# The MLP's up projections in a three-layer block: high and low part of h in one moving operand

## The reference

```python
def sq_relu_mlp(h, w1, w2):
    return jnp.square(jax.nn.relu(h @ w1)) @ w2      # w1: 1024 x 4096, w2: 4096 x 1024

# in each of the first two layers
h = rmsnorm(x, g[2])
x = x + rmsnorm(sq_relu_mlp(h, mlp_w1[l], mlp_w2[l]), g[3])
```

## Time and profile before

| | us |
|---|---|
| median of 3 runs (lowest, highest) | 912.43 (911.15, 913.14) |
| profiled execution, its time | 911.07 |
| profiled execution, span in the trace | 909.3 |
| PE busy in the span | 898.6 (99%) |
| DVE, ACT busy | 630.7 (69%), 483.4 (53%) |
| mean granted clock of PE | 0.997 of full speed |

### The profile page before, as it was taken

One profiled execution on the slowest core, in us unless ns is written; L12 is line 12 of the kernel. 1 busy time (PEld: TensorE's weight loads), 2 busy tenths in 40 slices (PEclk: granted clock), 3 DMA queues, 4 the chain that ended last, 5 costly groups with the idle time before them and its releaser, 6 DMA issues.

```text
span 909.3 us, 14541 instructions
## 1 busy us (share of the span) xinstructions
PE 898.6 (99%) x6258; PEld 796.2 (88%) x6258; DVE 630.7 (69%) x763; ACT 483.4 (53%) x639; POOL 33.6 (4%) x25
## 2 busy tenths in 40 slices
PE   8999999999999999999999999999999999999997
PEld 6989888899999998998889999999889998888885
DVE  5798746568666666689466867666678795456655
ACT  7775456465343334665566534334467784356624
POOL 0000000000000000000000000000000084000000
PEclk9999999999999999999999999999999999999999
DMA  9644544466666665544446666666445444334431
GB/s 352 238 171 139 179 142 142 140 215 226 231 231 231 232 232 185 176 173 139 139 139 215 229 228 232 236 233 233 149 168 209 140 139 141 98 112 145 140 133 46
DMA packets 24447, 165.47 MB, mean 182 GB/s; under 512 B 2720, under 2 KB 2976, under 8 KB 5184
## 3 DMA queue, kind: packets, MB, share of 16 engines
q1 hardware_dynamic: 22896, 159.72, 49.9%
q0 software_dynamic: 1056, 4.34, 1.3%
q10 hardware_dynamic: 432, 0.49, 0.2%
HBM read 163.49 MB, written 1.05 MB: 181 GB/s over the span
## 4 chain that ended last, share of the span: by engine, by line
PE 95%; DVE 2%; ACT 2%; DMA 1%; issue 0%; SPq 0%; DVEq 0%; ACTq 0%
PE acc L591 29%; PE lin L549 10%; PE lin L557 10%; PE lin L550 9%; PE lin L573 7%; PE lin L580 7%; PE lin L574 7%; PE acc L673 2%; PE acc L677 1%; PE acc L773 1%; PE acc L674 1%; PE lin L636 1%; PE acc L868 1%; DMA raw<-in_weights 1%; PE lin L651 1%; DVE w_lo L1792 1%
## 5 line engine op out<-in xcount | busy, mean ns | idle before, releaser
L1792 DVE TENSOR_TENSOR w_lo<-raw,w_hi 128x2048 fp32r<-128x2048 f32 x137 | 315.5, 2311 | 155.0 <-ACT w_hi L1309 154.4
L1309 ACT CAST w_hi<-raw 128x2048 fp32r<-128x2048 f32 x137 | 260.1, 1905 | 166.3 <-DMA raw<-in_weights 109.3
L549 PE MATMUL lin<-h_hi,w_hi 128*128 128x256 f32 x720 | 176.3, 286 | 0.0
L550 PE MATMUL lin<-h_lo,w_hi 128*128 128x256 f32 x720 | 174.7, 283 | 0.0
L549 PEld LDWEIGHTS lin<-h_hi,w_hi 128*128 128x128 f32 x720 | 137.9, 192 | 0.6
L550 PEld LDWEIGHTS lin<-h_lo,w_hi 128*128 128x128 f32 x720 | 138.2, 192 | 0.3
L591 PE MATMUL acc<-w_hi,f_hi 128*128 128x512 f32 x288 | 112.7, 391 | 0.0
L591 PE MATMUL acc<-w_hi,f_lo 128*128 128x512 f32 x288 | 112.3, 390 | 0.0
L573 PE MATMUL lin<-w_hi,h_hi 128*128 128x512 f32 x272 | 109.3, 402 | 0.1
L574 PE MATMUL lin<-w_hi,h_lo 128*128 128x512 f32 x272 | 106.3, 391 | 0.0
L557 PE MATMUL lin<-h_hi,w_lo 128*128 128x256 f32 x720 | 93.7, 283 | 0.0
(11 more groups left out here) (355 smaller groups left out, 1161.8 us busy)
## 6 DMA issues: line engine op xcount, KB each, us to landing
raw<-in_weights SPq DMA_DIRECT2D x149, 1024.0 KB, 4.9
rowbuf<-in_rows POOLq DMA_DIRECT2D x6, 512.0 KB, 4.2
x<-in_x_in SPq DMA_DIRECT2D x4, 256.0 KB, 4.4
raw<-in_weights SPq DMA_DIRECT2D x2, 512.0 KB, 6.9
arena<-in_const_even POOLq DMA_DIRECT2D x1, 1024.0 KB, 10.5
out<-x SPq DMA_DIRECT2D x3, 256.0 KB, 2.1
cst<-in_const SPq DMA_DIRECT2D x1, 576.0 KB, 8.3
out<-x ACTq DMA_DIRECT2D x1, 256.0 KB, 2.0
```

Source lines behind the costliest of these rows:

```text
L549: pe.matmul(o, hi[:, w], h[0], start=b == 0 and k == 0, stop=False)
L550: pe.matmul(o, hi[:, w], h[1], start=False, stop=False)
L1309: act.copy(w_hi[:, o % SPLIT, :], raw[:, j % RAW, :]).then_inc(hi_done, 1)
L1792: dve.tensor_tensor(w_lo[:, j % RAW, :], r, hi.bitcast(F32), ALU.subtract).then_inc(tile_split, 1)
```

## The change

The up blocks 1 to 7 of both MLPs are computed by a new function, `project_both_parts`. h_hi and h_lo lie side by side in one tensor `h_both`, so that one matmul of 512 columns moves both past the same stationary `w_hi`; the 256 columns of the high part and the 256 of the cross product land in different halves of a bank. The product with `w_lo` is added to the high half as before. A tile of 256 features now fills a whole pair, so that a block uses a pair for each of its tiles, and the list of `plan_lin` names them `up{l}_{i}.0` and `up{l}_{i}.1`. On reading, ACT copies the cross half to `arena` (`cross(j)`), DVE adds it to the other half, which frees the pair, and after both tiles DVE takes the maximum with 0 times the scales within `arena`. The transposed `up{l}_0` goes to `acc` and no longer has a place in the list. The last two parts of the diff are `mlp` of ACT and `mlp` of DVE.

```diff
         for i in range(8):
             if i < 7:
-                out.append(f"up{l}_{i + 1}")
-            if i == 0:
-                out.append(f"*up{l}_0")
+                out += [f"up{l}_{i + 1}.{j}" for j in range(2)]
             if ada_summed(l, i):
                 out.append("*" + ada_summed(l, i))
...
-        h_hi = sb("h_hi", [P, 12, T], F32R)
-        h_lo = sb("h_lo", [P, 12, T], F32R)
+        h_both = sb("h_both", [P, 12, 2, T], F32R)
+        h_hi, h_lo = h_both[:, :, 0, :], h_both[:, :, 1, :]
...
+            def project_both_parts(name, j):
+
+                n = FIRST[name] + j
+                out = f"{name}.{j}"
+                open_pair(out)
+                hi = high_tile(n)
+                for b in range(2):
+                    for k in range(DC):
+                        chunk(k)
+                        pe.matmul(pair(out)[:, b * 512:(b + 1) * 512], hi[:, k * 256 + b * P:k * 256 + (b + 1) * P],
+                                  h_both[:, k, :, :].rearrange("p a t -> p (a t)"), start=k == 0, stop=False)
+                lo = low_tile(n)
+                for b in range(2):
+                    for k in range(DC):
+                        mm = pe.matmul(pair(out)[:, b * 512:b * 512 + T], lo[:, k * 256 + b * P:k * 256 + (b + 1) * P], h_hi[:, k, :],
+                                       start=False, stop=k == DC - 1)
+                mm.then_inc(tile_used, 1)
...
                     if i == 0:
-                        project_feature_major(f"up{l}_1", (0,))
+                        project_both_parts(f"up{l}_1", 0)
                         broadcast_r()
-                        lead_turned(f"up{l}_0")
-                        project_feature_major(f"up{l}_1", (1,))
+                        lead_turned(acc).then_inc(turned_back, 1)
+                        project_both_parts(f"up{l}_1", 1)
                         after(r_ready)
                     elif i < 7:
-                        project_feature_major(f"up{l}_{i + 1}")
+                        for j in range(2):
+                            project_both_parts(f"up{l}_{i + 1}", j)
...
                     if i == 0:
-                        filled(act, name)
-                        act.copy(r, pair(name)[:, :]).then_inc(freed(name), 1)
-                    read_out(act, name)
+                        after(turned_back)
+                        act.copy(r, acc[:, 0:1024]).then_inc(relu_ready, 1)
+                    else:
+                        for j in range(2):
+                            act.wait_ge(tile_used, ORDINAL[FIRST[name] + j] + 1)
+                            act.copy(cross(j), part_of_pair(f"{name}.{j}", 1)).then_inc(cross_read, 1)
+                    act.wait_ge(relu_ready, 8 * l + i + 1)
...
                     if i > 0:
-                        filled(dve, name)
                         at = 8192 + (i % 2) * 1024
-                        dve.scalar_tensor_tensor(arena[:, at:at + 1024].rearrange("p (c t) -> p c t", c=4),
-                                                 pair(name)[:, :].rearrange("p (c t) -> p c t", c=4), 0.0, every,
-                                                 ALU.max, ALU.mult).then_inc(freed(name), 1)
-                    read_out(dve, name)
+                        for j in range(2):
+                            after(cross_read)
+                            ins = dve.tensor_tensor(arena[:, at + j * 512:at + (j + 1) * 512].rearrange("p (b t) -> p b t", b=2),
+                                                    part_of_pair(f"{name}.{j}", 0), cross(j), ALU.add)
+                            ins.then_inc(freed(f"{name}.{j}"), 1)
+                        for j in range(2):
+                            read_out(dve, f"{name}.{j}")
+                        z = arena[:, at:at + 1024].rearrange("p (c t) -> p c t", c=4)
+                        dve.scalar_tensor_tensor(z, z, 0.0, every, ALU.max, ALU.mult).then_inc(relu_ready, 1)
+                    dve.wait_ge(relu_ready, 8 * l + i + 1)
```

More of the change, by code:

```diff
@@ L233 @@
 WARM, WARM_UP = 11264, 16
+CROSS = 12288
 SUMS = ["ev_out", "down0_7", "od_out", "down1_7", "out"]
@@ L387, in build @@
         half_done = sem("half_done")
+        turned_back = sem("turned_back")
+        relu_ready = sem("relu_ready")
+        cross_read = sem("cross_read")
         by_done = sem("by_done")
@@ L435, in pair, with part_of_pair, cross @@
             return lin[LIN[name] % 2]
+        def part_of_pair(name, a):
+            return pair(name)[:, :].rearrange("p (b a t) -> p b a t", b=2, a=2)[:, :, a, :]
+        def cross(j):
+            return arena[:, CROSS + j * 512:CROSS + (j + 1) * 512].rearrange("p (b t) -> p b t", b=2)
         def freed(name):
@@ L732, in last_lead @@
                 project_token_major("dz", (0,), (1,))
-                lead_turned("dk")
+                lead_turned_in_pair("dk")
                 after(wg_ready)
@@ L746, in broadcast_r, with lead_turned @@
                 mm.then_inc(rb_done, 1)
-            def lead_turned(name):
+            def lead_turned(out):
                 after(z_out, 2)
-                open_pair(name)
                 for c in range(4):
@@ L755, in lead_turned, with lead_turned_in_pair @@
                         z = LEAD["z"] + t * 512 + c * P
-                        mm = pe.transpose(pair(name)[:, at:at + P], arena[:, z:z + P], ident)
-                mm.then_inc(lin_special, 1)
+                        mm = pe.transpose(out[:, at:at + P], arena[:, z:z + P], ident)
+                return mm
+            def lead_turned_in_pair(name):
+                open_pair(name)
+                lead_turned(pair(name)).then_inc(lin_special, 1)
             def chunk(k):
@@ L981, in _ @@
             broadcast_r()
-            lead_turned("mq")
+            lead_turned_in_pair("mq")
             project_feature_major("mk")
```

## The result

| | us |
|---|---|
| forecast for the median (range) | 947.3 (938.0 to 955.0) |
| changed kernel, median of 4 runs (lowest, highest) | 946.73 (946.26, 947.97) |
| kernel before, median of 4 runs | 911.83 (911.15, 913.14) |
| ratio, 95% interval | 1.0386, 1.0373 to 1.0398 |
| profiled execution of the changed kernel, its time and span | 947.97, 946.2 |

What follows compares the result with a forecast made beforehand. PE was taken as the bound, busy 898.6 of 909.3 us and never waiting inside the MLPs. 911.07 - 5.8 + 32.7 + 8.0 = 946.0, as a median 947.3 us; range 938 to 955.

Steps and rivals of the forecast that it cites:

- products: 448 fewer matmuls: Up blocks of both MLPs: 448 times a matmul's fixed part of 12.9 ns is saved, 5.8 us less.
- four waits for ada's pair: PE before four up tiles waits for DVE's ada reading: 9.4, 9.55, 9.2 and 4.55, together 32.7 us.
- clock behind the waits: PE after each of four waits: clock falls, costing 2.0 us each, 8.0 in all; bounds 0 and 9.6.
- reading, last f, transposes: MLPs: added ACT copies and DVE additions stay covered, transposes to acc cost nothing; 0, other end 0.3 us.
- Rival 2: Up blocks: waits come, but wider matmuls save nothing; median 953.1 us, 954.7 with clock at upper bound; chance 0.09.
- Rival 3: At the four places pairs come free in time and the saving stands; median 906.6 us; chance 0.03.
- Rival 1: At the four places the waits come but the clock holds; median 939.3 us; chance 0.13.
- The cover of the last f: End of second MLP: of 1.52 us room, new copy and addition take 1.27; cost 0, other end 0.3 us.
- rival 4: End of second MLP: the last f's cover is missed; some tenths of a us more, inside the range; no chance given.

Runs made afterwards that it cites:

- two-matmul experiment: The early reading kernel with two matmuls of 256 columns in place of each one of 512 past w_hi; 912.89 us, ratio 1.0011.
- early reading: Changed kernel with DVE reading the ada columns after the up block's own tiles are split, before splitting ahead; 907.26 us, ratio 0.9944.
- filled kernel: Changed kernel with 512-column matmuls that nothing reads issued before each of the four waiting tiles; 940.60 us, ratio 1.0314.
- second series: Changed kernel as it is, timed and traced again; 949.12 us, ratio 1.0405.
- one-split kernel: Changed kernel with the ada columns read after the second down tile's split, before that of the next up block's first tile; 919.89 us, ratio 1.0087.

## Why the prediction was right

The mechanism came as forecast: new places in the rotation, four waits behind the reading of the ada columns, a lower clock behind them, and the small saving of the matmuls. The profiled execution of the changed kernel is 947.97 - 911.07 = 36.9 us longer than that of the kernel before. Both traces have the same matmuls outside the up blocks, so the distance between the starts of the same matmul in the two shows where the time is gained or lost:

| step | predicted | measured, by starts |
|---|---|---|
| products: 448 fewer matmuls | -5.8 | -5.6 |
| four waits for ada's pair | +32.7 | +32.9 |
| clock behind the waits | +8.0 | +7.9 |
| reading, last f, transposes | 0 (0.3) | +0.7 |
| the start of the program | not forecast | +0.7 |
| the hybrid layer | not forecast | +0.2 |
| sum | +34.9 | +36.8 |

**The products.** The fixed part of a matmul, 12.9 ns, was read from two kinds of matmul that never stood side by side before, and it added up as it should: 5.54 us for a tile against 5.54 worked out. A stage saves 0.41 us, and 0.34 in the first of each MLP. The two-matmul experiment, 5.6 us slower, is the direct test. Rival 2, a wider matmul that gives nothing, falls. The Trainium skill ("TensorE: Matmul & The Clock Gate", section "Back-to-back issue gap") gave an estimated 1.1 us, and the measurement decides against it here: a fixed part of 2.5 ns does not fit these float32r matmuls.

**The waits.** Place, number and length came as worked out: 9.2, 9.1, 4.4 and 9.1 us against 9.4, 9.55, 4.55 and 9.2. The trace counts an idle time from the modelled end of the last matmul, 0.16 us after the next could start. From start to start the four are 32.4 us, and a tile behind a wait takes 0.1 us more than its neighbours even at full clock (5.68 against 5.57), which makes 32.9. The early reading takes all four away, and reading one split earlier leaves 2.9 of each long one. Rival 3, on the other side, was the right mechanism for another kernel: its 906.6 is the early reading's 907.26.

**The clock.** The size was taken from one case at the start of the program, 1.7 to 2.4 us, and at 2.0 a place it was near. (The Trainium skill, "TensorE: Matmul & The Clock Gate", section "HAM oscillation — how this bites in real kernels", has matmuls begin slow behind waits for loads. The trace agrees at the three long waits, which have a load in their chain: the clock is 0.50 when PE resumes. The start of the trace of before is less of an agreement than I made it: PE resumed at 12.32 with the clock at 1.00, and it fell at 13.7.) Rival 1, a clock that holds, falls: the filled kernel shows the 7.9 us. The loss differs by place (2.6, 1.6, 1.6, 2.1 us), more than my upper end of 2.4 at one of them. Why a place has the share it has, the runs leave open. That four places came to 8 us is luck in part.

**The cover of the last f** (rival 4). I gave 1.52 us of room and 1.27 of new work, and 0.3 as the other end. A wait of 0.3 us came, one step further on than I had looked. f itself is in time, and the split that is queued behind it on DVE is late. Before and after:

```profile
...
644.68 2.29 DVE L1792 TENSOR_TENSOR w_lo<-raw,w_hi 128x2048 fp32r<-128x2048 f32 x1 [0.42 <-ACT w_hi L1309]
...
647.91 0.62 PE L591 MATMUL acc<-w_lo,f_hi 128*128 128x512 f32 x2
...
```

```profile
...
682.13 2.29 DVE L1828 TENSOR_TENSOR w_lo<-raw,w_hi 128x2048 fp32r<-128x2048 f32 x1 [0.42 <-ACT w_hi L1341]
...
684.47 0.73 PE L619 MATMUL acc<-w_lo,f_hi 128*128 128x512 f32 x2 [0.31 <-DVE w_lo L1828]
...
```

The split ended at 646.97 and was wanted at 647.91. These 0.94 us were the narrower room, and the 1.27 of new work is 0.33 more. By starts the last down block loses 0.7 us, 0.5 of it at this wait. It is there in the early-reading kernel too.

**The start.** The same matmul of the first weight tile, in the trace of before and in that of after:

```profile
...
18.17 2.08 PE L839 MATMUL lin<-h_hi,w_lo 128*128 128x256 f32 x16
...
```

```profile
...
18.86 2.08 PE L871 MATMUL lin<-h_both,w_lo 128*128 128x256 f32 x16
...
```

This is the 0.7 us. Behind it stand larger differences that nearly cancel: the clock was low for 6.1 us of PE's work and not 3.4, the waits were 3.6 against 2.7 us, and the first sixteen matmuls took 5.34 in place of 6.43 us. The runs don't show whether the change has a part in it. What speaks against one: the fall of the clock at the start lasts 0 us in the two-matmul kernel, which has the changed layout, and 3.4 or 6.8 in the other traces, and the runs of the kernel before alone go from 909.95 us at a mean clock of 1.000 to 912.79 at 0.994. The cause of the 0.2 us in the hybrid layer is open.

**How near the forecast was.** The medians are 946.73 - 911.83 = 34.9 us apart, which is the forecast's sum to the tenth. Luck is in that: the second series of the same kernel is 37.2 us above the kernel before, and the terms that I had at nothing add 1.6 us to the sum in the traces.

## What to carry to other kernels

When a change gives one user of a double buffer more places in the rotation, list the order of places anew and ask of each, two places back, what its reading is queued behind. A reader of four columns that costs 0.15 us held up TensorE for 9 us, because it stood in its queue behind work that begins only when TensorE gets there; the trace of before had the whole chain in it, at full length and harmless. Put the small reading ahead of the large work, and the gain that the change was worth comes out: 907.26 us against 912.1 before and 946.7 after.

## What the runs showed of the hardware

Behind gaps of 2.9 us the clock fell in two cases of three in the one-split kernel. PE resumed at 300.2, the clock fell at 301.7 and was low for 3.4 us; behind the third gap it was low for 3.4 us too. The tiles there take 7.29 and 7.19 us in place of 5.68, a loss of 1.6 and 1.5 us on top of the wait. **A short wait can cost half as much again**, then, and whether it does is not settled by its length.

**The clock fell with PE busy.** In three traces, the filled, the two-matmul and the one-split kernel, the granted clock went to 0.50 for 3.4 us in the odd layer, where PE waits for nothing. It follows eight matmuls whose stationary operand has 4 partitions. In the timeline and the windows of the filled kernel:

```profile
...
436.65 1.97 PE L1014 MATMUL lin<-arena,cst 4*128 4x256 f32 x8
...
439.52 0.63 PE L609 MATMUL lin<-w_hi,h_both 128*128 128x512 f32 x1
439.95 0.63 PE L608 MATMUL lin<-w_hi,h_both 128*128 128x512 f32 x1
...
```

```profile
...
439.00:440.00 1.00, 1.00 (x5) 0.57 0.95 401
440.00:441.00 1.00, 1.00 (x4) 0.50 0.78 328
442.00:443.00 1.00, 1.00 (x5) 0.72 0.00 0
...
```

While the clock is low, matmuls of 512 columns start 0.43 us apart, where they start 0.227 apart at full clock. That is less than twice: a low stretch loses 47% of its length in such matmuls, not half. So 3.4 us cost 1.6.

With these eight issued three times over:

```profile
...
414.22 7.31 PE L1005 MATMUL lin<-arena,cst 4*128 4x256 f32 x24
...
```

```profile
...
417.00:418.00 1.00, 1.00 (x6) 0.80 1.06 451
418.00:419.00 1.00, 1.00 (x4) 0.50 0.24 98
...
424.00:425.00 1.00, 1.00 (x5) 0.79 0.00 0
...
```

The clock falls at 417.6, while they still run, and is low for 6.8 us. The time, 914.37, is the early reading's 907.26 plus 3.8 for the added matmuls plus some 3.3, about half of the low stretch, as far as sums of medians go, and the mean clock of all ten runs is 0.991 to 0.993 where the early reading's five have 0.994 to 0.998. In the traces of the kernel before (with either order of reading), the changed kernel (both) and the early reading the eight ran without a fall, so at that length it hangs on something else too, which the runs leave open. Nor do they show what it is about these matmuls: the 4 partitions are one of the things in which they differ from their neighbours. An engine that is never idle in the timeline can still find its clock halved.
